# A decoder layer with expert retrieval on one Trainium2 core: projection passes regrouped, the first tile's experts chosen two heads at a time

## The reference

```python
xn = rmsnorm(x, norm_mix_w)
proj = xn @ w_in                       # 2816 columns: q, k, v of the attention, q, f, i, g of HGRN2
attn = sliding-window attention (8 heads of 64, 2 key heads, window 128, T5 bias table, sinks)
o_h = HGRN2 in chunks (4 heads of 128 x 128 state), normed, times silu(g)
h = x + concat(attn, o_h) @ w_o
hn = rmsnorm(h, norm_ffn_w)
# PEER: 8 heads, 2 x 128 sub-keys each, top 16 of each half, top 16 of the sums
eidx, gate = top 16 experts and softmax of their scores, per token and head
act = gelu(einsum('thkd,td->thk', u[eidx], hn))
y = h + einsum('thk,thkd->td', gate * act, v[eidx])
```

## Time and profile before

| | |
|---|---|
| median of 3 runs | 3186.58 us (3182.06 to 3189.6) |
| profiled execution | 3190.91 us |
| its span | 3188.8 us |
| Tensor engine busy | 2593.6 us (81%) |
| Vector engine busy | 2397.5 us (75%) |
| Scalar engine busy | 1524.5 us (48%) |
| GpSimd busy | 2069.0 us (65%) |
| DMA | 1214.05 MB, mean 381 GB/s |

### The profile page before, as it was taken

One profiled execution on the slowest core, in us unless ns is written; L12 is line 12 of the kernel. 1 busy time (PEld: TensorE's weight loads), 2 busy tenths in 40 slices (PEclk: granted clock), 3 DMA queues, 4 the chain that ended last, 5 costly groups with the idle time before them and its releaser, 6 DMA issues. The chain is left out here.

```text
span 3188.8 us, 34779 instructions
## 1 busy us (share of the span) xinstructions
PE 2593.6 (81%) x8357; PEld 1380.7 (43%) x8357; DVE 2397.5 (75%) x5775; ACT 1524.5 (48%) x4133; POOL 2069.0 (65%) x2162
## 2 busy tenths in 40 slices
PE   7997899878977988688967887678767885778967
PEld 6853545445444544354434433343334432443321
DVE  2457777777887877887778878896888778776684
ACT  3415642366346643574346643573348433543333
POOL 1106575666766676667766777767776776676765
PEclk9999999999999999999998999999989999999989
DMA  8519999999999999999999999999999999999998
GB/s 289 196 46 350 361 409 381 412 404 410 400 403 395 410 409 409 388 410 409 407 382 390 401 409 409 394 392 409 409 399 386 405 408 409 367 408 410 409 393 341
DMA packets 360948, 1214.05 MB, mean 381 GB/s; under 512 B 43867, under 2 KB 70460, under 8 KB 359452
## 3 DMA queue, kind: packets, MB, share of 16 engines
q0 software_dynamic: 308288, 1121.46, 89.2%
q1 hardware_dynamic: 24588, 57.77, 4.8%
q10 hardware_dynamic: 27872, 32.61, 2.9%
HBM read 1191.24 MB, written 21.46 MB: 380 GB/s over the span
## 5 line engine op out<-in xcount | busy, mean ns | idle before, releaser
L1237 PE MATMUL ps<-rows,diag 128*128 128x256 f32 (+2 forms) x4224 | 1634.5, 518 | 515.8 <-DMA rows<-in_peer_v,idx 369.3
L1680 DVE CUSTOM_DVE_ANT_0 rows<-rows,ps 128x1024 f32<-128x1024 f32 x1056 | 1281.9, 1214 | 440.2 <-DMA rows<-in_peer_u,idx 437.6
L592 POOL DMA_INDIRECT rows<-in_peer_v,idx x1056 | 1022.3, 968 | 524.1 <-issue 241.0
L576 POOL DMA_INDIRECT rows<-in_peer_u,idx x1056 | 1021.6, 967 | 478.6 <-issue 245.9
L1237 PEld LDWEIGHTS ps<-rows,diag 128*128 128x128 f32 (+1 forms) x4224 | 752.4, 193 | 1269.2 <-issue 816.5
L869 ACT ACTIVATE act_g<-act_g 128x1 f32<-128x1 f32 x1056 | 211.9, 201 | 1196.1 <-DVE act_g L1680 1178.5
L1691 DVE SCALAR_TENSOR_TENSOR resid<-rows,act_g,resid 128x256 f32<-128x256 f32 x1024 | 493.4, 482 | 6.2 <-ACT diag L877 6.2
L877 ACT ACTIVATE diag<-ident,act_g 128x128 f32<-128x128 f32 x1024 | 411.3, 402 | 104.3 <-PE ps L1237 72.5
L873 ACT ACTIVATE act_g<-act_g,gate 128x1 f32<-128x1 f32 x1056 | 311.0, 294 | 34.3
L1116 PE MATMUL ps<-w_sc,r 128*128 128x512 f32 (+1 forms) x576 | 284.4, 593 | 0.9 <-DVE w_sc L1332 0.9
L987 PE MATMUL ps<-rows,bias 128*128 128x384 f32 (+1 forms) x608 | 211.2, 501 | 0.0
(11 more groups left out here) (291 smaller groups left out, 1886.3 us busy)
## 6 DMA issues: line engine op xcount, KB each, us to landing
bias<-in_w_in ACTq DMA_DIRECT2D x38, 512.0 KB, 6.8
rows<-in_peer_u,idx POOLq DMA_INDIRECT x1056, 9.4
rows<-in_peer_v,idx POOLq DMA_INDIRECT x1056, 9.4
r<-proj SPq DMA_DIRECT2D x7, 1344.0 KB, 8.8
w_sc<-in_w_q_t SPq DMA_DIRECT2D x8, 1024.0 KB, 8.5
proj<-staged ACTq DMA_DIRECT2D x41, 192.0 KB, 9.3
rows<-in_w_in POOLq DMA_DIRECT2D x14, 512.0 KB, 3.9
w_o<-in_w_in POOLq DMA_DIRECT2D x10, 512.0 KB, 6.3
```

What stands on the lines that cost most here:

```text
L576: nc.gpsimd.indirect_dma_start(ring[:, slot, :], None, a["peer_u"], bass.IndirectOffsetOnAxis(ap=idx[g % 2][:, k:k + 1], axis=0), engine_s ...
L592: nc.gpsimd.indirect_dma_start(ring[:, slot, :], None, a["peer_v"], bass.IndirectOffsetOnAxis(ap=idx[g % 2][:, k:k + 1], axis=0), engine_s ...
L1237: last = nc.tensor.matmul(Y[j][0:m, lo:512], diag[:, n % DIAGS, 0:m], ring[:, slot, 512 * j + lo:512 * (j + 1)], start=(k == 0), stop=(k = ...
L1680: V.tensor_tensor_reduce(ring[:, slot, :], ring[:, slot, :], hn_u, 1.0, 0.0, ALU.mult, ALU.add, col).then_inc(S["dots"], 1)
```

## The change

1. **Passes.** Pass 1 is tiles 0 and 1 as before, pass 2 tiles 2, 3 and the sample (288 columns), pass 3 tiles 4 to 7 (512 columns). Period -1 has no block; periods 0, 1, 2 have 22, 11 and 11. A block of pass 3 is copied out and stored in two parts, at one and at three steps after it, each when the store before has landed. The chunks of weights stay in slots 12 and 13, the bias stays on chip and is loaded once.
2. **Ring.** `u` has 5 slots in tile 0 and 4 in tiles 1 and 2, `v` has 5 in tiles 0 to 2; from tile 3 on it is 8 and 7.
3. **Choice for tile 0** in four groups of two heads, each with its own `idx_done` and `topk_done`: group 0 in period -1 right after the first quarter of the scores, the heads of group 1 at its end, the rest of group 1 and groups 2 and 3 in steps 0 to 29 of period 0, beside the dots. `hn_u` is computed before group 0.
4. **Folds.** The last four sub-key sets are folded after three quarters of the scores.
5. **Front of tile 1** starts in period 0 (`TIMES_SECOND`) from the first five chunks; the other 16 are loaded when the last group has read its scores.
6. **Side columns.** Tile 0: none up to step 47 (the Tensor engine adds 1024 columns), then 512 (the Tensor engine adds 512). Tiles 1 and 2: 384 (and 640). Then 256 as before.
7. `TIMES_NEAR` now holds up to tile 4, `TIMES_FAR` from tile 5.

The core of the diff:

```diff
-U_SETS = {0: (0, 1, 2, 3, 12), 1: (8,), 4: (9, 10)}
-V_SETS = {0: (4, 5, 6, 7, 14, 13), 4: (11,)}
+GROUPS = 4
+GHEADS = PH // GROUPS
+GPICKS = PICKS // GROUPS
+U_SETS = {0: (0, 1, 2, 3, 8), 3 * PICKS: (8, 9, 10, 12)}
+V_SETS = {0: (4, 5, 14, 6, 7), 3 * PICKS: (11, 13)}
+U_LENT = {PICKS: (8,)}
-SIDE, SIDE_LAG = 2 * P, 3
+SIDE_LAG, SIDE_FROM = 3, 48
-PASS2 = 3 * P + NS
-PASS3 = 3 * P
+PASS2 = 2 * P + NS
+PASS3 = 4 * P
-BLOCK_AT = {-1: [96 + 2 * b for b in range(6)],
-            0: [28, 31, 34, 37, 77, 81, 84, 88, 91, 95, 98, 102, 106, 110, 114, 118],
-            1: [28, 32, 36, 78, 84, 90, 96, 102],
-            2: [8, 12, 16, 20, 74, 82, 90],
-            3: [8, 12, 16, 20, 74, 80, 86]}
-FOLD_AT = [40 + 2 * c for c in range(2 * PH)]
+BLOCK_AT = {0: [26, 29, 32, 35, 38, 41, 44, 47, 86, 88, 91, 93, 96, 98, 101, 103, 106, 108, 111, 113, 116, 118],
+            1: [28, 32, 36, 77, 83, 89, 95, 101, 107, 113, 119],
+            2: [28, 32, 36, 77, 82, 88, 93, 99, 104, 110, 115]}
+FOLD_AT = [40 + 2 * c for c in range(12)] + [90, 91, 92, 93]
...
+TIMES_FIRST |= {TOP + x: t for x, t in enumerate((79, 80, 96, 97, 133, 136, 146, 149))}
+TIMES_FIRST |= {G_CAND + g: t for g, t in enumerate((81, 128, 140, 151))}
+TIMES_FIRST |= {G_PICK + g: t for g, t in enumerate((82, 130, 142, 154))}
+TIMES_FIRST |= {G_GATE + g: t for g, t in enumerate((95, 131, 144, 156))}
+TIMES_FIRST |= {G_GATED + g: t for g, t in enumerate((98, 132, 145, 157))}
...
+def side_of(g, k):
+    if is_sample(g):
+        return 0
+    return (4 * P if k >= SIDE_FROM else 0) if g == 0 else 3 * P if g < 3 else 2 * P
...
             def load_proj(f):
-                sp.wait_ge(S["sc_done"], f)
                 if f == 1:
...
+                    sp.dma_start(pj[:, 0:5, :], proj[f, :, 0:5, :]).then_inc(S["proj_in"], 16)
...
+                    sp.wait_ge(S["sc_done"], f)
+                    sp.dma_start(pj[:, 5:CHUNKS - 1, :], proj[f, :, 5:CHUNKS - 1, :]).then_inc(S["rest_in"], 16)
+                    return
...
-                if f >= 2 and f - 2 in BLOCK_AT:
-                    sp.wait_ge(S["block"], blocks_before(f - 1, 0))
-                    load_bias()
...
-                pool.wait_ge(S["idx_done"], g + 1)
...
+                    if g == 0 and k < PICKS and k % GPICKS == 0:
+                        pool.wait_ge(S["idx_done"], k // GPICKS + 1)
...
+            def keep_later(b, part):
                 c, j = b % CHUNKS, b % 2
+                bank, pair = F[2 + j], slice(2 * P * part, 2 * P * (part + 1))
+                if part == 0:
+                    act.wait_ge(S["block"], b + 1)
+                    if b + 2 < LATER:
+                        act.dma_start(wp[j], a["w_in"][(b + 2) % CHUNKS]).then_inc(S[f"w_b{j}"], 16)
+                if b or part:
+                    act.wait_ge(S["proj_out"], stores_before(b) + 16 * part)
...
-                for j in range(2):
-                    lo = SIDE if j == 0 and not is_sample(g) else 0
+                side = side_of(g, k)
+                for j in range(side // 512, 2):
+                    lo = side if j == 0 else 0
...
+            def choose(k, g):
...
+                if k == G_PICK + g:
...
+                    V.scalar_tensor_tensor(idx[0][:, picked], pos_g[0], float(P), pos_g[1], ALU.mult, ALU.add).then_inc(S["idx_done"], 1)
```

More of the change, by code:

```diff
@@ L196, in blocks_before, with stores_before, chosen, sides_until @@
     return sum(q < p or (q == p and x < k) for q in BLOCK_AT for x in BLOCK_AT[q])
[L199 to L209, removed]
+def stores_before(b):
+    return 32 * b
+def chosen(f):
+    return GROUPS + f
+def side_of(g, k):
+    if is_sample(g):
+        return 0
+    return (4 * P if k >= SIDE_FROM else 0) if g == 0 else 3 * P if g < 3 else 2 * P
+def sides_until(n):
+    return sum(side_of(x // PICKS, x % PICKS) > 0 for x in range(n + 1))
+def ring_table(sets, lent):
     order, before, uses, out = [], [None] * RING, [0] * RING, []
     for n in range(PICKS * TILES + PICKS // SGRP):
-        if n % PICKS == 0:
-            order = list(sets.get(n // PICKS, ())) + order
+        order = list(sets.get(n, ())) + [x for x in order if x not in lent.get(n, ())]
         slot = order.pop(0)
@@ new lines, in keep_later @@
+                last = nc.scalar.activation(out, bank[:, pair], ACT.Copy)
+                if b < CHUNKS or part:
+                    last.then_inc(S["kept_b"], 1)
+                    act.wait_ge(S["kept_b"], b + 1)
+                else:
+                    own.mark(last)
+                    own.settle()
+                first = 2 if b < CHUNKS else 4 + 2 * part
+                act.dma_start(proj[first:first + 2, :, place(c), :].rearrange("i p t -> p i t"),
+                              out.rearrange("p (i t) -> p i t", t=P)).then_inc(S["proj_out"], 16)
@@ L995, in turn, with spread_norm @@
                 return last
+            def spread_norm(g, f):
+                if g is None:
+                    pe.wait_ge(S["kept"], CHUNKS)
+                    pe.wait_ge(S["consts_in"], 16 * 10)
+                else:
+                    pe.wait_ge(S["dots"], PICKS * (g + 1))
+                for c in range(DC):
+                    last = nc.tensor.matmul(hn_u[:, P * c:P * (c + 1)], w_ffn_t[:, c:c + 1].to_broadcast([P, P]), ident[:, :],
+                                            start=True, stop=True)
+                last.then_inc(S["w_spread"], 1)
             def front(k, f):
@@ L1266, in _ @@
                 for k in [*steps(p), *range(PICKS, PICKS + SUM_LAG)]:
-                    if f is not None and k == (PICKS if f else BLOCK_AT[-1][0]):
+                    if f and k == PICKS:
                         spread_norm(g, f)
```

300 lines of the change are left out of this document (194 added, 106 removed).

## The result

| | before | after |
|---|---|---|
| median of 12 runs | 3188.16 us (3182.06 to 3193.84) | 3200.36 us (3193.88 to 3212.64) |
| profiled execution | 3190.91 us | 3193.88 us |
| its span | 3188.8 us | 3192.1 us |
| DMA | 1214.05 MB, mean 381 GB/s | 1210.90 MB, mean 379 GB/s |

The ratio of the medians is 1.0039, with an interval from 1.0028 to 1.0051: the change makes the kernel 12 us **slower**. I had said 3167. The profiled execution of the changed kernel happens to lie 6.5 us under its median, so between the two profiles only 3.3 us of span remain. The places are the same in a second profile (run e15).

The account below looks back on a forecast made before the run. The DMA stream of gathers, full at about 409 GB/s, was taken as the bound. Terms -31.6 + 3.6 + 10 + 8.2 + 10.2 - 19.9 gave -19.5 us, a median of 3167, range 3145 to 3194.

Parts of the forecast that it names:

- Start, -31.6: Before the first dot: earlier scores and choice put the first gather near 206 us, first dot at 221.5, not 253.1.
- Steps 0 to 48 of tile 0, +3.6: Vector engine bounds steps 0 to 30 (85 us), then 64 us to step 48, against 145.4 before.
- Steps 48 to 128, +10: Tile 0: 231 us of bytes plus 14 for the Scalar engine's store waits, 245 against 234.8; range -4 to +30.
- The rival in which the stores pace tile 0: Landings stay at 10 us, 13 intervals take 10.7: 265 instead of 245, total 3187, no change; chance 0.17.
- Tile 3, -19.9: 7 blocks and a bias load gone, -14.9 us of bytes, and 5 of 8 us of other loss won back.
- Tiles 4 to 8, 0: Same ring and bytes as before, so no change in time.
- Tiles 1 and 2, +8.2 and +10.2: More bytes, 3.2 and 6.2 us, plus 5 us a tile for shorter rings and 384 side columns.
- I take 5 and 4: Tiles 1 and 2: loss beside bytes from late gathers after Vector engine bursts, between zero and 20 us a tile.
- a sign of being wrong: The forecast counts as wrong if, among other signs, tiles 1 and 2 grow by over 30 us together.
- The ring: Tiles 1 and 2: a u slot's round of 9.1 us just fits four steps of 10.25, with 1.1 us to spare.
- The stores: Tile 0, steps 48 to 128: Scalar engine waiting for store landings costs 0 to 34 us beyond bytes; taken as 14.
- The rival of the short ring: Tiles 1 and 2: from a landing of 8.7 us bursts are lost in full, 44 us instead of 9, 3202; chance 0.16.

Follow-up runs that it names:

- e15: The changed kernel itself, unaltered, run again with a second profile: 3198.33 us, 1.0029 of the kernel before.
- e2: The changed kernel with 256 side columns in tiles 1 and 2 in place of 384: 3200.02 us, 1.0029.
- e3: The changed kernel with later blocks' weights in the bias tile, bias read again twice, slots 12 and 13 idle, ring still 4 and 5: 3213.79 us, 1.0073.
- e4: e3 with slots 12 and 13 given to the ring in tiles 1 and 2 (5 u, 6 v): 3188.56 us, 1.0000.
- e5: e3 with slot 12 given to the u slots in tiles 1 and 2 (5 and 5), slot 13 idle: 3201.62 us, 1.0046.
- e6: e5 with four staging buffers in slot 13, so a copy waits for the store four before: 3186.92 us, 0.9998.
- e7: The changed kernel with 2 diagonals in place of 3: 3229.01 us, 1.0136.
- e8: e7 with a 512-column staging tile, each half's copy waiting only for its own last store: 3201.83 us, 1.0048.
- e16: e3 with four staging buffers in slot 13, ring of 4 and 5, on a slow chip: 3457.46 us, 0.9920 of the kernel before there.
- e17: e3 run again on the slow chip of e16: 3477.89 us, 0.9999 of the kernel before there.
- e13: e4 with block copies 2 and 5 steps after the block and tile 2's blocks six steps apart (e11 again, usual chip): 3179.16 us, 0.9971.
- e1: The kernel before with 4 u and 5 v slots in tiles 1 and 2 in place of 6 and 6: 3204.22 us, 1.0041.
- e9: The changed kernel with second copies 4 steps after the block and tile 2's blocks six steps apart, on a slow chip: 3487.04 us, 1.0020.
- e11: e4 with copies 2 and 5 steps after the block and tile 2's blocks six steps apart, on a slow chip: 3475.58 us, 0.9984.
- e18: e4 with second copies 4 steps after the block and tile 2's blocks six steps apart, on the slow chip of e16: 3481.44 us, 1.0003.

## Why the prediction was wrong, point by point

- **Start, -31.6: right.** -32.9 by the first dots. Gather at 205.1 for 206, first dot at 220.3 for 221.5, last scores from 214.3 for 215.4.
- **Steps 0 to 48 of tile 0, +3.6: right.** 84.9 and 65.3 against 85 and 64, so +4.8.
- **Steps 48 to 128, +10: right.** 242.6 for 245, and the 14 stores from 477.9 to 595.0 us stand 9.0 apart, as I had it. The stores of tile 0 land in 6.7 us in the median and those of the sample's columns in 8.0, less than the 10 of before: as I had half supposed, a queue that runs shorter lands sooner. The rival in which the stores pace tile 0 falls (it had 265).
- **Tile 3, -19.9: right**, -18.8. **Tiles 4 to 8, 0: right**, 2.0 us less altogether.
- **Tiles 1 and 2, +8.2 and +10.2: wrong**, +19.7 and +24.6. The step that failed is "I take 5 and 4" for what they lose beside their bytes. The two tiles grew by 44.3 us where I had 18.4, and by over 30, which I had named as a sign of being wrong. The side columns were sized rightly (620 ns), and giving them back gained nothing (e2). The bytes were 1.5 MB too high in tile 1 and right in tile 2. Two terms were missing or too small:
  - *The ring.* I let a `u` slot turn in 9.1 us, under the 10.25 of four steps, and said it just fits. The gathers landed in 7.0 us in the median, no later than I had assumed, and the ring still cost time. A median says nothing of the late ones: the longest landing in that stretch is 11.5 us, and with the 1.6 of dot and semaphores its round is 13.1, over the 10.25. That the late ones make the cost is my reading; no run has them alone. My 7.5 came from 39 us of tile 0 with 5 `u` slots; in tile 1 of the same trace the median is 10.4 and the longest 17.4, so the "6 us to spare" of six slots were not there either. Two slots were worth 25 us (e3 to e4); a ring of 4 and 5 alone, in the kernel before, cost 14 by the medians, and 11 in the two tiles of its profile.
  - *The stores.* I costed the Scalar engine's wait for landings in tile 0, at 14 us, and left it out of tiles 1 and 2, though the diff makes two stores of each block out of one there, the second three steps behind the block through one overlapping buffer. By itself that wait costs 15 us with 5 and 5 slots (e5 to e6), 27 with 4 and 5 and two diagonals (e7 to e8), and 20 with 4 and 5 on the slow chip (e16, e17).
- The two can't be added: 25 and 15 are more than the 26 us that were missing, and e3, from which the 25 are counted, is itself 11 us over the changed kernel. No run takes both away: e13, 33 us under e3 by the ratios, has the longer ring but most of the landing wait, and e6 has no landing wait but 5 and 5 slots. How the 26 us divide between the two is therefore open.
- **The rival of the short ring** named the place, the sign and nearly the time (3202). Its threshold was wrong, a landing of 8.7 us, since at 7.0 the loss is there, and it gave the ring 35 us over my 9, where e1 shows 14 and stores, which it did not have, made a part. That its time comes within 2 us of 3200 is luck.
- The page "Perfetto Trace Analysis" of the Trainium skill, section "Optimization Strategy", says that one gap repeating on the engine that should be full can mean too few buffers. The rows agree: steps 48 to 64 of tile 1, without a block, show 390 for 409 GB/s, and slots raised the rate of the tile (375 in e3, 388 in e4). But a lower rate is no proof of a short ring: without a slot more, taking away the wait for a store raised it as well (381 in e5, 392 in e6).

The landings of `u` gathers, minimum, median and maximum, in 640 to 990 us of the kernel before, and in 620 to 990 us of the changed one:

```profile
DMA to landing us min/median/max: 6.6/10.4/17.4
```

```profile
DMA to landing us min/median/max: 4.2/7.0/11.5
```

## What to carry to other kernels

Where a stream is to be kept full through a ring, the landing time measured with many buffers doesn't tell whether fewer are enough: the landing shrinks with the number in flight and the rate goes with it. So take slots away and measure (e1 changes four lines), and best in the kernel that will have the ring: 14 us in the kernel before became 25 for two slots in the changed one. The idle time by releaser doesn't price a slot either (57 us in e1, 3 in e5). An engine that computes for the stream and also issues stores should not wait for the last store's landing in front of the stream's work: give each store in flight its own buffer. Here one slot given to that was worth as much as one given to the ring (e6, e4), and on a slow chip it was worth 20 us where longer rings gained nothing that can be told. And a wait that the diff makes in three places has to be costed in all three.

## What the runs showed of the hardware that I had not expected

- **Landing and rate go together.** In tile 1 a gather of `u` lands in 10.4 us with 12 slots at 405 GB/s (the kernel before), in 7.6 with 9 at 391 (e1), in 7.0 with 9 at 384 (the changed kernel). A 128 KB store lands in 7.0 us in the median of the changed kernel. The page "DMA: Bandwidth & Descriptors" of the Trainium skill, section "Anatomy of one DMA — SWDGE (gpsimd) path", has some 2.0 us of fixed cost for a DMA and its bytes over 436,000 beside it, an estimate of 3.2 us for a 512 KB gather. No gather of `u` in these stretches landed so soon: the shortest took 6.6 us with 12 slots and 4.2 with 9. So the time to plan with is the one from a row.
- **Chips differed by 9%.** On two of the chips that the runs fell on, the kernel before took 3476 (e9 to e11) and 3478 us (e16 to e18), on the others 3187 to 3190. The undisturbed tile 4 of e9, to be set beside the 403 GB/s at 1.02 of the changed kernel above:

```profile
1841.70:2227.30 385.60, 281.62 (x809) 153.83 (x807) 281.34 (x682) 174.20 (x477) 245.47 (x256) 0.87 0.95 356
```

  There the same kernel with the short ring (e3 and e17) is level with the kernel before (0.9999), where it is 1.0073 elsewhere, while the wait for the landing costs no less (20 us for 15, with another ring). So what a slot is worth differs between chips; the lower rate goes with it, and whether it is the cause is not shown, nor what makes the rate lower there.
- **The mean clock of a tile did not go with its time.** The granted clock, whose full level is 2.4 GHz and whose other is 1.2, averages 0.89 in tile 1 of the changed kernel for 0.98 before, with TensorE busy 321 of 388 us for 300 of 368. In e13 it is 0.90 and the tile is 11 us shorter; in e2 it is 0.95, with more columns on TensorE, and the tile is no shorter. No run changes the clock alone.
